# Modulation sums on TensorE in four column quarters, in a two-block transformer kernel

## The reference, cut to what matters

```python
mod = c_act @ w_mod + b_mod                      # c_act = silu(c), w_mod 1024 x 3072, per layer
shift, scale, gate = jnp.split(mod[:, None, :], 3, axis=-1)
h = rms_norm(x, pre_gain) * (1.0 + scale) + shift
proj = h @ w_in                                  # 1024 x 3088
...
y = jnp.concatenate([a_out, r_out, g_out], axis=-1) @ w_out
return x + gate * rms_norm(y, post_gain)
```

## Time and profile before

| what | us |
|---|---|
| median of three runs (2828.62 to 2842.18) | 2834.99 |
| the profiled execution | 2828.72 |
| its span, first to last instruction | 2826.9 |
| TensorE busy (matmuls) | 2348.4 |
| VectorE busy | 1387.5 |
| GpSimd busy | 1094.7 |
| ScalarE busy | 870.1 |
| mean granted clock of TensorE | 0.907 |

### The profile page before, as it was taken

The page is one execution under the profiler, slowest core; times in us unless marked ns, Lnnn a source line. Parts: engine busy times, 40 slices in busy tenths (PEclk is TensorE's granted clock), DMA queues, the critical chain, the costliest instruction groups (busy, mean ns, idle before and its releaser), DMA issues. The chain is left out here.

```text
span 2826.9 us, 32109 instructions
## 1 busy us (share of the span) xinstructions
PE 2348.4 (83%) x12450; PEld 1926.9 (68%) x12450; DVE 1387.5 (49%) x2051; ACT 870.1 (31%) x1568; POOL 1094.7 (39%) x793
## 2 busy tenths in 40 slices
PE   2888657988556879788949999999779899799997
PEld 2677435777435765466749898999668667588886
DVE  4875563795552856445854251223358774300012
ACT  2214113214113127465142121111231584422222
POOL 1433325433325324132264343333454243555444
PEclk9999668989768979799969999999889999899999
DMA  6441011540011420000513132323134000133331
GB/s 233 160 140 34 1 45 56 182 128 23 1 53 56 132 76 2 0 8 4 180 37 113 56 110 81 105 82 116 60 121 138 23 2 25 57 97 97 97 97 67
DMA packets 147727, 218.87 MB, mean 77 GB/s; under 512 B 18484, under 2 KB 71124, under 8 KB 147448
## 3 DMA queue, kind: packets, MB, share of 16 engines
q1 hardware_dynamic: 147576, 216.82, 24.2%
HBM read 214.69 MB, written 2.10 MB: 77 GB/s over the span
## 5 line engine op out<-in xcount | busy, mean ns | idle before, releaser
L284 POOL TENSOR_TENSOR w_lo<-w_raw,w_hi 128x1024 fp32r<-128x1024 f32 (+3 forms) x252 | 593.9, 2358 | 1061.2 <-ACT w_hi L277 1061.1
L277 ACT ACTIVATE w_hi<-w_raw 128x1024 fp32r<-128x1024 f32 (+3 forms) x252 | 255.6, 1017 | 1194.9 <-PE ps L297 982.0
L295 PE MATMUL ps<-w_hi,h_transposed 128*128 128x512 f32 (+3 forms) x1088 | 418.1, 384 | 57.7 <-POOL w_lo L284 22.0
L296 PE MATMUL ps<-w_lo,h_transposed 128*128 128x512 f32 (+3 forms) x1088 | 409.7, 377 | 0.0
L297 PE MATMUL ps<-w_hi,h_transposed 128*128 128x512 f32 (+3 forms) x1088 | 408.9, 376 | 0.0
L295 PE MATMUL ps<-h_transposed,w_hi 128*128 128x384 f32 (+1 forms) x1056 | 373.8, 354 | 2.5 <-issue 2.1
L296 PE MATMUL ps<-h_transposed,w_hi 128*128 128x384 f32 (+1 forms) x1056 | 373.3, 353 | 0.0
L297 PE MATMUL ps<-h_transposed,w_lo 128*128 128x384 f32 (+1 forms) x1056 | 373.1, 353 | 0.0
L355 DVE SCALAR_TENSOR_TENSOR mod_acc_aux<-w_raw,c_act,mod_acc_aux 128x512 f32<-128x512 f32 x280 | 278.4, 1019 | 44.2 <-DMA w_raw<-in_w_mod_dram 22.3
L295 PEld LDWEIGHTS ps<-w_hi,h_transposed 128*128 128x128 f32 x1088 | 213.4, 196 | 101.6 <-POOL w_lo L284 27.5
L1311 DVE TENSOR_TENSOR ffn_full<-ps,ffn_silu 128x768 f32<-128x768 f32 (+1 forms) x44 | 34.2, 819 | 422.2 <-PE ps L297 422.2
(11 more groups left out here) (303 smaller groups left out, 3621.8 us busy)
## 6 DMA issues: line engine op xcount, KB each, us to landing
w_raw<-in_ada_w_dram SPq DMA_DIRECT2D x96, 512.0 KB, 4.3
w_raw<-in_ffn_w_in_dram SPq DMA_DIRECT2D x88, 512.0 KB, 3.6
w_raw<-in_w_mod_dram SPq DMA_DIRECT2D x48, 512.0 KB, 4.6
w_raw<-in_ffn_w_out_dram SPq DMA_DIRECT2D x44, 512.0 KB, 3.6
w_raw<-in_w_in_dram SPq DMA_DIRECT2D x40, 512.0 KB, 4.6
w_raw<-in_w_out_dram SPq DMA_DIRECT2D x16, 512.0 KB, 4.8
w_raw<-in_od_w_in_dram SPq DMA_DIRECT2D x16, 512.0 KB, 4.7
mod_gain<-in_norm_g_dram SPq DMA_DIRECT2D x16, 256.0 KB, 4.0
```

The costliest lines, as they stand in the source:

```text
L277: act.activation(w_hi[:, i % 2, 0:k * n], w_raw[:, u % 4, 0:k * n], ACT.Copy).then_inc(w_hi_ready.sem, 1)
L284: pool.tensor_tensor(w_lo[:, i % 2, 0:k * n], w_raw[:, u % 4, 0:k * n], w_hi[:, i % 2, 0:k * n].bitcast(F32), ALU.subtract).then_inc(w_lo_ ...
L295: pe.matmul(acc, left[0], right[0], start=start, stop=False)
L296: pe.matmul(acc, left[0], right[1], start=False, stop=False)
```

## The change

The sums of 24 jobs (those in the five `Linear` stages A to E) move from VectorE to TensorE; the jobs at the start and in `FeedForward` stay where they are (`by_pe=False`). `c_act` becomes 32 columns wide, zero but for columns 1 and 2, which hold the two vectors. `pe_sum` multiplies four feature tiles at a time, feature tile g into partitions 32g to 32g + 31 of bank 6, so that the four use four column quarters of the array. It is called twice per job, behind the quarters 1 and 3 of a chunk with one job, and behind every quarter in a chunk with two. The two slots of a call come free together when it ends. `collect` on VectorE adds the bias row in row 0 and multiplies the gain; for the last job of a chunk it stands behind the copies. `turn` then sums with `c_pick`, a column that picks row 0 and the rows 32g + 1 + r; it uses bank 7 alone, waits for the copy of the turn before, and stands behind quarter 0 of the next chunk. For shift and scale it is four matmuls for both vectors.

Besides: in C `rotate_q` goes from chunk 1 to chunk 2; in the first block `FirstWeights` (two weight splits) leaves the `Work` phase before `MixTransposed` and becomes an entry of its own behind it; and three probability buffers lie elsewhere, because the static tiles have grown.

```diff
-STATIC_COLS, STATIC_W = _layout([("ident", P), ("ones", P)])
+STATIC_COLS, STATIC_W = _layout([("ident", P), ("ones", P), ("picks", 2)])
...
+    row = np.arange(P)
+    t[:, slice(*STATIC_COLS["picks"])] = np.stack([(row == 0) | (row % 32 == 1 + r) for r in range(2)], 1)
...
-        c_act = static("c_act", [P, 2, KT, 2])
+        c_act = static("c_act", [P, 2, KT, 32])
...
+            def pe_sum(self, pe, half):
+
+                if half == 0 and self.n:
+                    pe.wait_ge(mod_collected.sem, self.n)
+                cond = self.conds[0][0]
+                units = [ring["mod"][4 * self.k + 2 * half + i] for i in range(2)]
+                for i, u in enumerate(units):
+                    pe.wait_ge(w_landed[u % 4].sem, 16 * (u // 4 + 1))
+                    for j in range(2):
+                        g = 2 * i + j
+                        ins = pe.matmul(ps[32 * g:32 * g + 32, 6, :], c_act[:, cond, 4 * half + g, :], w_raw[:, u % 4, j * HALF:(j + 1) * HALF],
+                                        start=(half == 0), stop=(half == 1))
+                ins.then_inc(mod_unit.sem, 2)
+
+            def collect(self, dve):
+                first = self.bias_row(dve)
+                dve.wait_ge(mod_unit.sem, 4 * self.k + 4)
+                ins = dve.tensor_tensor(self.acc[:, 0], ps[:, 6, :], first, ALU.add)
+                ins.then_inc(mod_collected.sem, 1)
+                dve.wait_ge(mod_collected.sem, self.n + 1)
+                self.times_gain(dve, 1)
...
-                    if m >= 2:
-                        pe.wait_ge(mod_kept.sem, m - 1)
+                    if m:
+                        pe.wait_ge(mod_kept.sem, m)
                     if self.kind == "gate":
-                        ins = pe.matmul(ps[:, 6 + m % 2, :], ones, self.acc[:, r], start=True, stop=True)
+                        if self.by_pe:
+                            ins = pe.matmul(ps[:, 7, :], c_pick[:, r:r + 1].to_broadcast([P, P]), self.acc[:, 0], start=True, stop=True)
+                        else:
+                            ins = pe.matmul(ps[:, 7, :], ones, self.acc[:, r], start=True, stop=True)
...
                         ins.then_inc(w_used.sem, 1)
-                    if first == 0 and jobs:
-                        wait_bank(pe, self.source, 6)
-                        wait_bank(pe, self.source, 7)
+                        if q == 0:
+                            for job in before:
+                                job.turn(pe)
+                        if q == 0 and first == 0 and jobs:
+                            wait_bank(pe, self.source, 6)
+                            wait_bank(pe, self.source, 7)
+                        if jobs and len(jobs) == 1 and q % 2:
+                            jobs[0].pe_sum(pe, q // 2)
+                        if len(jobs) == 2:
+                            jobs[q // 2].pe_sum(pe, q % 2)
                     first += len(tiles)
-                    for job in jobs:
-                        job.turn(pe)
+                    before = jobs
+                for job in before:
+                    job.turn(pe)
...
-                    for job in jobs:
-                        for q in range(4):
-                            job.sum(dve, q)
+                    for job in jobs[:-1]:
+                        job.collect(dve)
                     for step in self.beside["dve"].get(c, []):
                         step(dve)
...
                         i += 1
+                    for job in jobs[-1:]:
+                        job.collect(dve)
...
-            first_weights = FirstWeights()
-            schedule.append(Work(dve=dve, pool=pool, sp=prelude_sp, act=first_weights.scalar))
+            schedule.append(Work(dve=dve, pool=pool, sp=prelude_sp))
+            schedule.append(FirstWeights())
...
-            linear.beside["dve"] = {1: [rotate_q], 2: [latent_meansq, latent_norm]}
+            linear.beside["dve"] = {2: [rotate_q, latent_meansq, latent_norm]}
```

More of the change, by code:

```diff
@@ L205, in build @@
         window = static("window_bf16", [P, 2 * P], BF16)
-        small_at, SMALL = place[0], 5696
+        small_at, SMALL = place[0], 5216
         arena = small_at + SMALL
@@ L302, in build, with __init__ @@
         mod_ready = signal("mod_bias_cleared")
+        c_cleared, mod_collected = signal("c_cleared"), signal("mod_sums_on_pe")
         turns_before = []
         class ModJob:
-            jobs = turns = 0
-            def __init__(self, w, bias, kind, gain, conds, targets, half, col, acc):
+            jobs = turns = on_pe = 0
+            def __init__(self, w, bias, kind, gain, conds, targets, half, col, acc, by_pe):
                 self.k, ModJob.jobs = ModJob.jobs, ModJob.jobs + 1
@@ L321, in __init__ @@
                 turns_before.append(self.turn0)
+                self.by_pe = by_pe
+                if by_pe:
+                    self.n, ModJob.on_pe = ModJob.on_pe, ModJob.on_pe + 1
                 self.side_bias = mod_side[self.k % 2].plan(16) + 16
@@ L339, in load, with bias_row, times_gain @@
                              self.w[q * 256:(q + 1) * 256].rearrange("(k p) n -> p k n", p=P)).then_inc(w_landed[u % 4].sem, 16)
-            def sum(self, dve, q):
[L343 to L349, removed]
+            def bias_row(self, dve):
+                first = mod_bias[:, self.k % 2, :]
+                dve.wait_ge(mod_side[self.k % 2].sem, self.side_bias)
+                if self.k >= 2:
+                    dve.wait_ge(mod_turned.sem, turns_before[self.k - 1])
+                if self.kind == "scale":
+                    dve_s.chain(dve.tensor_scalar(first[0:1, :], first[0:1, :], 1.0, None, ALU.add))
+                return first
+            def times_gain(self, dve, n):
+                if self.gain is not None:
+                    dve.wait_ge(mod_side[2].sem, self.side_gain)
+                    dve.tensor_tensor(self.acc[:, 0:n], self.acc[:, 0:n], mod_gain[:, :].unsqueeze(1).to_broadcast([P, n, HALF]), ALU.mult)\
+                       .then_inc(mod_summed.sem, 1)
+                else:
+                    dve.drain().then_inc(mod_summed.sem, 1)
+            def sum(self, dve, q):
+                first = self.bias_row(dve) if q == 0 else None
                 i = 4 * self.k + q
@@ L362, in sum @@
                 if q == 3:
[L363 to L369, removed]
+                    self.times_gain(dve, len(self.conds))
+            def pe_sum(self, pe, half):
[17 more added lines that the diff above has]
+                self.times_gain(dve, 1)
             def turn(self, pe):
@@ L671, in tensor @@
             def tensor(self, pe):
-                first = 0
+                first, before = 0, []
                 for (c0, n, tiles), jobs in zip(self.chunks, self.mods):
@@ L1476, in act @@
                 eng.wait_ge(early_landed.sem, 16 * len(early))
-                for cond, r, raw in ((0, 0, 0), (0, 1, 0), (1, 0, 1), (1, 1, 2)):
-                    eng.activation(c_act[:, cond, :, r], c_raw[:, raw, :], ACT.Silu)
+                eng.wait_ge(c_cleared.sem, 1)
+                for cond, r, raw in ((0, 0, 0), (1, 0, 1), (1, 1, 2)):
+                    eng.activation(c_act[:, cond, :, 1 + r], c_raw[:, raw, :], ACT.Silu)
             def dve(eng):
                 eng.memset(mod_bias[:, :, :].rearrange("p b n -> p (b n)"), 0.0).then_inc(mod_ready.sem, 1)
+                eng.memset(c_act[:, :, :, :].rearrange("p c k n -> p (c k n)"), 0.0).then_inc(c_cleared.sem, 1)
                 eng.memset(minus_half[:, :], -0.5)
```

44 lines of the change are left out of this document (25 added, 19 removed).

## The result

Measured beside each other, the kernel before takes 2833.8 us (median of 4, 2828.62 to 2842.18) and the changed one 2943.9 (median of 4, 2942.41 to 2946.49): a ratio of 1.0386, 95% interval 1.0366 to 1.0406. The forecast was 2922, with a range of 2870 to 2985. The profiled execution of the changed kernel took 2942.4 with a span of 2940.6, 113.7 more than the profiled one before.

A forecast was written before the change was run, and what follows sets the result against it. VectorE's sums delayed its copies, but TensorE idled only about 19, 19, 16, 2 and 8 us in A to E; ring waits would cost more. Terms sum to +87 on 2828.7, 2916; median 6.3 higher, 2922, range 2870 to 2985.

The forecast's parts named there:

- rival 1: The forecast itself: weights wait in the ring, column quarters run side by side, clock partly down; chance 0.79.
- Half a chunk, 16.75: A and B, 512 columns: 8.7 from modulation issue to first matmul, 5.45 quarter, 1.2 call, 1.4 clock loss.
- rival 2: Loads come in time, the lead staying under quarter 2: 512-column chunk 25.1, A 153, whole kernel 2810; chance 0.10.
- The 272-column chunk, 24.4: Chunk in A and B: two halves of 6.7 lead, 2.9 quarter, 1.2 call and 1.4 clock loss.
- The last chunk, 12.1: A and B's last chunk, 256 columns and no job: four quarters of 2.8 and a turn.
- First chunk, 29.1: First chunk of A and B: quarter 3 starts later, +5.2, so 29.1 where it took 23.9.
- E, +29.2: Odd projection: +5.2, +7.9, +10.8 and +3.1 in its chunks, +2.2 in VectorE's tail.
- C, -5: Even projection: late copy and w_lo waits, clock loss and half the turns' matmuls go; eight calls of 1.2 come.
- D, +5: Even output: calls +9.6, less wait -1.8, clock -3.4 and turns -1.8; one-bank gate turns and last collect +2.7.
- FeedForward, +2.4: Sums stay; with one bank the second turn of each of four parts waits some 0.6 for a copy.
- FirstWeights, -8.3: First-block Work phase: moving the weight splits out saves 4.2 us a layer, the split hidden under transposes.
- The third: Rival: the column quarters of a call do not overlap; +106, 3028 us in all; chance 0.07.

The follow-up runs named there:

- run 1: Changed kernel with the ring issuing W0 W1 M0 M1 W2 W3 M2 M3 (W weights, M modulation) in one-job chunks; 2820.3 us, ratio to before 0.994.
- run 2: Changed kernel, ring order untouched, with a two-matmul call behind every quarter in one-job chunks, four calls instead of two; 2851.7 us, ratio to before 1.0065.
- run 7: Kernel before, all sums on VectorE, with FirstWeights moved (run 4) and the weights-first ring order of run 1; 2828.1 us, ratio to before 0.9966.
- run 3: Changed kernel with the sums of A, B and E back on VectorE, C and D still on TensorE; 2828.7 us, ratio to before 0.9977.
- run 10: Changed kernel with the turns of jobs summed on VectorE going through two banks, 6 and 7, again; 2940.5 us, ratio to before 1.0373.
- run 4: Kernel before with only FirstWeights moved, to a stage of its own behind the Work phase; 2826.2 us, ratio to before 0.9967.
- run 5: Kernel of run 1 with the four matmuls of a call one after the other on the first column quarter; 2930.9 us.
- run 6: Changed kernel, ring untouched, with three matmuls of zeros behind the first call of each one-job chunk, filling idle time; 2922.0 us.

## Why the prediction was right, and where it was off

The mechanism was the forecast's (rival 1), and each of its links is in the trace: a modulation and a weight unit issued together behind each call, a lead of 8.69, twelve waits in A and in B, no wait for a copy there. Runs 1 and 2 took the waits away by two different edits, and the time went with them; run 7 shows that the order did nothing before the sums moved.

The profiled execution is 113.7 us above the one before, and the forecast said 87. So the sum was 27 us too small; most of that lies in A and B. By its own steps:

- *Half a chunk, 16.75.* Measured 17.08 and 17.37 in turn (calls at 114.34, 131.42 and 148.79), 34.45 a chunk for 33.5. The first is 1.12 from the call to the issue (1.2 forecast for the call), 8.69 of lead (8.7), and 7.27 for the quarter with its clock loss (5.45 + 1.4). The pace of 5.45 holds for matmuls in a row (the chunk of run 1 is 25.11, and rival 2 had made 25.1 of 21.8, the turn and two calls), but behind a wait the quarter takes 5.7, and the clock 1.6. In the second half, with the turn in it, the lead is 8.8 to 9.2. Four chunks: +4.
- *The 272-column chunk, 24.4.* Two half-rate stretches of 6.8 us each lie in it; 26.8. +2.4.
- *The last chunk, 12.1.* This is a missing term. The second of its weight units takes the slot of a modulation unit that comes free with the last call, and the two behind it stand on the queue: the three are issued from 262.99 on, after that call. A wait of 1.18 and a stretch at 0.51 follow, 15.4 in all. +3.3.
- *First chunk, 29.1.* 30.2, +1.1. With the three above that is A: +44.8 by its window where +34.1 was forecast. B is the same stage again: +40.5 for +29.7.
- *E, +29.2.* Measured +30.0 (134.5 to 164.5, between its first and its last matmul), and this agreement is in part luck. The first chunk grew by 8.7 where 5.2 was forecast (a wait of 3.05 lies in it, and half-rate stretches of 3.4 us at 2166.6 and 2183.6), the next three by 7.8, 10.0 and 3.4 (7.9, 10.8, 3.1), and VectorE's tail, put at +2.2, grew by 0.1: its last copy ends 5.8 us behind TensorE's last matmul and did so 5.7 before.
- *C, -5.* Measured -3.6; *D, +5*, +4.2. In C the late copy (7.2) went, 1.8 is left of the 5.0 for `w_lo`, and the calls came, as worked out. TensorE waits 2.2 us for ScalarE's copies of gate turns (1.4 before). By the spread given under run 3, other profiles would have made this -2.4 to -6.2 for C and +4.2 to +5.9 for D.
- *FeedForward, +2.4.* +4.7: the bank is 2.4 of it (run 10), clock about 1, and the rest is open.
- *FirstWeights, -8.3.* The VectorE steps beside it are 4.15 shorter in each layer, 8.3 in all. The stretches between A, B and their output projections as wholes are 6.8 and 3.2 shorter, -10.0; alone -10 (run 4).
- *Between C and D*, +2.9 was not forecast and is not of the change: in run 4 the stretch took 304.5 us and in run 7 301.3, with the same code there, at a mean clock of 0.88 and 0.89. An execution has one half-rate stretch more or less in it.

The rivals. The second (loads in time, A at 153, the whole at 2810) is nearly what run 1 gave: 157.0, 155.1 and 2820.3; the excess is 10 us, in A (+4), B (+2), C and `FeedForward`. It was well priced, and its condition, a lead that fits the cover, is what failed. The third (quarters in turn, +106) is run 5: +110.6. For the fourth, a lead of 6.7 to 7, there is no run.

The Trainium skill ("TensorE: Matmul & The Clock Gate", Part 3, Measured speedup vs the span model) gave 2.38x for three column tiles. Here four took 1.07 where the same four in turn took 3.62, 3.4x by the records: with four tiles for three and at this shape, the trace is better than that figure. What the kernel pays is 1.22 for a call side by side (run 1) and 2.30 more in turn (run 5), 2.9x.

## What to carry to other kernels

In a ring that two consumers share and one queue fills in order, a unit is late when the one *issued ahead* of it waits for its slot, though its own slot has long been free. So when work moves to a consumer that gives slots back later, reorder the issues in the same edit: units whose slots come free early go first. Before moving work onto an engine, ask stage by stage whether it has idle time there (A, B and C had 16 to 19 us of it, D and E 2 and 8), and count what the new waits do to the clock: in A twelve waits took 33.0 us, and the half-rate stretch behind most of them took 1.6 more.

## What the hardware showed that was not expected

- A call of two float32 matmuls on two column quarters takes 1.05 us, one of four on four quarters 1.06 to 1.07, four in turn on one quarter 3.62.
- In the changed kernel each of the 24 waits for `w_lo` in A and B, 1.1 to 3.6 us long, has a stretch of 3.4 or 6.8 us at 0.50 at it or behind it. In run 6, where half of these waits were filled, waits of 2.17 to 2.48 us in B left the granted clock at 1.00, and waits of 2.24 to 2.85 in A did not. The length of a wait alone did not decide.
- A VectorE step on 256 columns takes 0.42 us with GpSimd idle and 2.55 while GpSimd makes `w_lo`; at the end of E in the changed kernel a step (L1140) that takes 0.82 took 3.05 and 2.90 at 2291.97 and 2298.63, beside `w_lo`s that began at 2291.95 and 2297.81.
